# Attention of a hybrid decoder step: products of weights and values placed alternately in the two column halves of TensorE's array

## What the reference computes

```python
p_c = masked_softmax(q @ kc, ends of the 32-token blocks <= position)   # compressed keys, 32 of them
p_s = masked_softmax(q @ k_slc, keys <= position)                        # selected keys: here all blocks up to the query
p_w = masked_softmax(q @ k_win, the last 512 keys)                       # window
out = g0 * (p_c @ vc) + g1 * (p_s @ v_slc) + g2 * (p_w @ v_win)          # g: a sigmoid gate per head and branch
```

## Time and profile before

| | us |
|---|---|
| median of 3 runs | 2473.39 (2472.95 to 2475.03) |
| the profiled execution, own time | 2473.83 |
| its span | 2472.0 |
| TensorE busy with matmuls | 2288.4 (93%) |
| TensorE busy with weight loads | 1726.6 (70%) |
| VectorE busy | 826.4 (33%) |
| ScalarE busy | 501.9 (20%) |
| GpSimd busy | 292.6 (12%) |

### The profile page before, as it was taken

The page is one execution under the profiler, slowest core; times in us unless marked ns, Lnnn a source line. Parts: engine busy times, 40 slices in busy tenths (PEclk is TensorE's granted clock), DMA queues, the critical chain, the costliest instruction groups (busy, mean ns, idle before and its releaser), DMA issues.

```text
span 2472.0 us, 30188 instructions
## 1 busy us (share of the span) xinstructions
PE 2288.4 (93%) x11143; PEld 1726.6 (70%) x11143; DVE 826.4 (33%) x1909; ACT 501.9 (20%) x1029; POOL 292.6 (12%) x274
## 2 busy tenths in 40 slices
PE   4979999996888888899999999898999999989998
PEld 1245567775655566566667766678999999978886
DVE  0131123247666666653211111552111111133343
ACT  2020001011333333321111011442111111123232
POOL 0000001101000000003200001530000000035543
PEclk9989999997999999999999999999999999999999
DMA  7620100101200000035341342431111111134553
GB/s 269 224 75 26 43 17 18 35 2 69 78 4 4 4 5 4 4 96 154 113 117 57 100 119 86 161 122 52 51 48 37 51 34 51 34 120 128 179 171 103
DMA packets 179724, 189.40 MB, mean 77 GB/s; under 512 B 10069, under 2 KB 149437, under 8 KB 179198
## 3 DMA queue, kind: packets, MB, share of 16 engines
q1 hardware_dynamic: 178590, 184.12, 23.8%
q10 hardware_dynamic: 1056, 4.23, 0.5%
HBM read 173.88 MB, written 16.53 MB: 77 GB/s over the span
## 4 chain that ended last, share of the span: by engine, by line
PE 77%; DVE 11%; issue 5%; ACT 3%; DMA 3%; DVEq 0%; ACTq 0%; SPq 0%; POOL 0%; PEldq 0%
PE ps L2173 20%; PE ps L2091 14%; PE ps L1774 8%; PE ps L1790 5%; PE ps L2139 4%; PE ps L2140 4%; PE ps L2141 4%; PE ps L1742 3%; PE ps L1968 3%; DVE arena L1368 2%; PE ps L1951 2%; PE ps L1927 1%; DVE arena L1389 1%; ACT arena L902 1%; DMA arena<-in_w_out 1%
## 5 line engine op out<-in xcount | busy, mean ns | idle before, releaser
L2173 PE MATMUL ps<-h_hi,wup_hi 128*128 128x344 f32 x1056 | 340.6, 323 | 18.5 <-PE ps L2173 11.2
L2173 PE MATMUL ps<-h_lo,wup_hi 128*128 128x344 f32 x1056 | 339.3, 321 | 0.0
L2173 PE MATMUL ps<-h_hi,wup_lo 128*128 128x344 f32 x1056 | 339.0, 321 | 0.0
L2139 PE MATMUL ps<-rw_hi,ra_hi 128*128 128x512 f32 x540 | 217.7, 403 | 17.4 <-DVE rw_lo L1550 11.3
L2173 PEld LDWEIGHTS ps<-h_hi,wup_hi 128*128 128x128 f32 x1056 | 199.5, 189 | 24.8 <-issue 24.2
L2140 PE MATMUL ps<-rw_hi,ra_lo 128*128 128x512 f32 x540 | 214.1, 397 | 0.0
L2141 PE MATMUL ps<-rw_lo,ra_hi 128*128 128x512 f32 x540 | 213.5, 395 | 0.0
L2091 PE MATMUL ps<-hT,arena 128*128 128x344 f32 x704 | 211.1, 458 | 0.0
L1774 PE MATMUL ps<-arena,hT 128*128 128x386 f32 (+1 forms) x576 | 190.2, 491 | 12.1 <-DMA arena<-in_w_in 12.1
L2173 PEld LDWEIGHTS ps<-h_lo,wup_hi 128*128 128x128 f32 x1056 | 199.4, 189 | 0.0
L2173 PEld LDWEIGHTS ps<-h_hi,wup_lo 128*128 128x128 f32 x1056 | 199.2, 189 | 0.0
(11 more groups left out here) (380 smaller groups left out, 2733.4 us busy)
## 6 DMA issues: line engine op xcount, KB each, us to landing
hT<-in_w_down SPq DMA_DIRECT2D x66, 512.0 KB, 3.5
arena<-in_w_ada SPq DMA_DIRECT2D x12, 2048.0 KB, 7.9
arena<-in_w_up SPq DMA_DIRECT2D x44, 512.0 KB, 4.9
arena<-in_w_in SPq DMA_DIRECT2D x30, 512.0 KB, 4.8
arena<-in_w_out SPq DMA_DIRECT2D x24, 512.0 KB, 3.6
arena<-in_cache_cmp_kv SPq DMA_DIRECT2D x64, 128.0 KB, 2.0
arena<-in_cache_slc_kv SPq DMA_DIRECT2D x128, 64.0 KB, 1.9
arena<-in_w_in SPq DMA_DIRECT2D x4, 1544.0 KB, 9.0
```

What stands on the lines that cost most here:

```text
L2139: nc.tensor.matmul(out, ra_hi[rnd][a][:, rows], rw_hi[rnd][w][:, cols], start=(k == 0), stop=False)
L2173: ins = nc.tensor.matmul(ps[:, bank, 0:TG], w[:, k0 + k, :], h[:, k, toks], start=(k == 0 and j == 0), stop=(k == KD - 1 and j == 2))
```

## The change

In `att_PV` the products of a query block alternate between partitions 0 to 63 and 64 to 127 of the bank, counted on from the "w" unit to the "s" unit, so that the bank holds two partial sums of 64 x 128. ScalarE's `att_out` moves the upper partial sum to one of two buffers `ohalf` in SBUF; it no longer waits for the transfer of `ost`, and waits instead that the buffer has been read. VectorE has an `att_out` of its own: it waits for that move (and, for the first query block, for the transfer of `ost`), adds both halves, and writes `ost`. On VectorE it stands behind max(u + 2) of even u of 2 and more; the one of the last query block stands behind the loop over u, ahead of the next head's max(0). To keep the number of semaphores, four of the sample part's semaphores become one that counts 1 to 4, at the same places.

```diff
+        ohalf = [Pm[0:HD, 6, j * P:(j + 1) * P] for j in range(2)]
...
+        s_oh = sem("att_half")
...
@@ ScalarE
             def att_out(i, h):
 
                 act.wait_ge(s_pv, h * NU + (2 * i + 2))
-                if i == 0:
-                    act.wait_ge(s_ybd, h * 16 + 16)
-                nc.scalar.activation(ost[:, i * P:(i + 1) * P], ps[0:HD, 6 + i % 2, 0:P], ACT.Copy).then_inc(s_comb, 1)
+                act.wait_ge(s_comb, h * NT + max(i, 1))
+                nc.scalar.activation(ohalf[i % 2], ps[HD:P, 6 + i % 2, 0:P], ACT.Copy).then_inc(s_oh, 1)
...
@@ VectorE
+            def att_out(i, h):
+
+                dve.wait_ge(s_oh, h * NT + (i + 1))
+                if i == 0:
+                    dve.wait_ge(s_ybd, h * 16 + 16)
+                nc.vector.tensor_tensor(ost[:, i * P:(i + 1) * P], ps[0:HD, 6 + i % 2, 0:P], ohalf[i % 2], ALU.add).then_inc(s_comb, 1)
+
...
+                    if u % 2 == 0 and u:
+                        att_out(u // 2 - 1, h)
+                att_out(NT - 1, h)
             own.end(NH)
...
@@ TensorE, att_PV
                 if kind == "w":
                     pe.wait_ge(s_comb, h * NT + max(i, 1))
+
+                at, last = (0 if kind == "w" else len(units[u - 1][3])), len(units[2 * i][3]) + i
                 for o, (c, w, b) in enumerate(blocks):
...
-                    ins = nc.tensor.matmul(ps[0:HD, 6 + i % 2, 0:P], v, src, start=(kind == "w" and o == 0),
-                                           stop=(kind == "s" and b == i))
+                    half = (at + o) % 2 * HD
+                    ins = nc.tensor.matmul(ps[half:half + HD, 6 + i % 2, 0:P], v, src, start=(at + o < 2), stop=(at + o >= last - 1))
                 ins.then_inc(s_pv, 1)
```

More of the change, by code:

```diff
@@ L384, in build @@
             sem(n) for n in ("pages_used", "pages_weighted", "pages_T", "pages_act", "pages_dve", "q_padded"))
[L385 to L388, removed]
+        s_sps, s_Qall, s_soft, s_softm, s_softe, s_sPT, s_sPTe = (
+            sem(n) for n in ("samples_ps", "Q_all", "soft", "soft_max", "soft_exp", "sPT_ps", "sPT"))
+        s_cg, s_cge, s_sWd, s_sWp, s_sh2, s_shd, s_sCn, s_sya = (
+            sem(n) for n in ("sm_gate", "sm_exp", "sm_W", "sm_W_ps", "sm_h", "sm_std", "sm_C", "sm_ya"))
+        SP_Q, SP_Y, SP_IMP, SP_O = 1, 2, 3, 4
         s_wmg, s_wl = ([sem(f"{n}{j}") for j in range(2)] for n in ("wmerge", "w_up"))
@@ L1436, in samples_dve @@
                 if n == 1:
-                    dve.wait_ge(s_Qps, 1)
+                    dve.wait_ge(s_sps, SP_Q)
                     for g in range(NKV):
@@ L1495, in samples_dve @@
                 if n == 10:
-                    dve.wait_ge(s_syT, 1)
+                    dve.wait_ge(s_sps, SP_Y)
                     nc.vector.tensor_copy(yaT[:, :, SEQ:TOK], ps[:, 5, 256:288].rearrange("p (b h) -> p h b", h=MH)).then_inc(s_sya, 1)
@@ L1512, in samples_dve @@
                 if n == 22:
-                    dve.wait_ge(s_impps, 1)
+                    dve.wait_ge(s_sps, SP_IMP)
                     step(nc.vector.tensor_reduce(imp, ps[0:SR, 4, 0:NCMP].rearrange("p (k r) -> p k r", r=2), AX.X, ALU.add))
@@ L1539, in samples_dve @@
                 if n == 32:
-                    dve.wait_ge(s_Osum, 1)
+                    dve.wait_ge(s_sps, SP_O)
                     for h in range(NH):
@@ L2004, in samples_pe @@
                         ins = nc.tensor.transpose(ps[:, 5, 64 + j * NS:64 + (j + 1) * NS], Ps[:, lo:lo + P], ident[0:NS, 0:NS])
-                    ins.then_inc(s_Qps, 1)
+                    ins.then_inc(s_sps, 1)
                 if n == 3:
@@ L2031, in samples_pe @@
                         pe.wait_ge(s_sh2, 2)
-                        nc.tensor.transpose(ps[:, 5, 256:288], hv, ident[0:32, 0:32]).then_inc(s_syT, 1)
+                        nc.tensor.transpose(ps[:, 5, 256:288], hv, ident[0:32, 0:32]).then_inc(s_sps, 1)
                     for j in range(NPAGE):
@@ L2041, in samples_pe @@
                     pe.wait_ge(s_soft, 2)
-                    nc.tensor.matmul(ps[0:SR, 4, 0:NCMP], cst("same_group", SR), pcm, start=True, stop=True).then_inc(s_impps, 1)
+                    nc.tensor.matmul(ps[0:SR, 4, 0:NCMP], cst("same_group", SR), pcm, start=True, stop=True).then_inc(s_sps, 1)
                 if n == 24:
@@ L2071, in samples_pe @@
                 if n == 32:
-                    nc.tensor.matmul(ps[:, 0, 0:SR], ones[0:1, :], zrow[:, 0:SR], start=False, stop=True).then_inc(s_Osum, 1)
+                    nc.tensor.matmul(ps[:, 0, 0:SR], ones[0:1, :], zrow[:, 0:SR], start=False, stop=True).then_inc(s_sps, 1)
             def scores(b):
```

## The result

The change makes the kernel slower: 2513.4 us median (2510.8 to 2518.5) against 2473.2, ratio 1.0163 (1.0149 to 1.0177), or 40 us. The forecast was 2495 with a range of 2486 to 2513; the time lies 0.4 us above it. The sign, the place and the largest term were right, and the sum was short by 18 us. The profiled execution took 2510.8, its span is 2509.0, 37.0 above the span before.

What follows compares the result with a forecast made beforehand. VectorE's and ScalarE's chain of max, exp and scale was taken to bound the middle of a head. +30.1 us there less 8.6 at the heads' ends gave +21.5 on 2473.39: 2495 us, range 2486 to 2513.

Steps and rivals of the forecast that it cites:

- What bounds the stage: Middle of a head: VectorE's and ScalarE's max, exp and scale in sequence set a unit's period, whatever TensorE does.
- The hold of 3.76 us a head: Even steps 2 to 12: VectorE's wait, addition and exposed copies delay scale(u + 2), 30.1 us over 8 heads.
- Full overlap: Products in different halves run side by side, n taking n + 1 steps for 2n; chance 0.56 with nearly full.
- The move ends at 690.75 as now (same size, same place in ScalarE's order): Step u = 6: ScalarE's move behind exp(8) keeps its time, seen by VectorE at 690.78, 0.16 behind scale's old start.
- 719.25 - 718.71 = 0.54: Head's end: shorter PV(13) lets T(15) start 0.54 us earlier, limited by scale(15).
- The passage, "gain 1.01 us": Between heads: PV(15) ends 1.82 us earlier, the table load after addition and max(0) 1.01 us earlier, at 7 passages.
- The clock: Rival 3: in the middle TensorE's clock falls once a head, some 2 us lost each, 2511 in total; chance 0.07.
- The signs in the new profile: Expected in the new profile: addition waits 0.8 to 1.4 us, TensorE waits over 100, 12 matmuls about 1.0, heads 2.7 longer.
- Rival 1: The halves don't overlap: TensorE keeps its pace, VectorE pays all, +36 us, 2510; chance 0.22.
- the addition's bounds: VectorE's addition, taken as 0.20 us, lies between 0.16 and 0.30; over 48 times -2 to +5 us.

Runs made afterwards that it cites:

- the better order: Changed kernel with additions in odd steps, no ScalarE buffer wait, each head's last addition between the next head's max(0) and max(1): 2466.6 us, ratio 0.9963.

## Why the prediction was right or wrong

The mechanism was right; what failed are four sizes in the sum: the start of ScalarE's move, the gain booked to PV(13), the length of the passage behind the addition, and the clock, put at nothing.

- **What bounds the stage**: right. VectorE's and ScalarE's chain sets the middle; freed TensorE time became idle (50.87 us a head with the halves alone, 50.88 before).
- **The hold of 3.76 us a head**: right. 3.73 with everything in the lower half.
- **Full overlap**: right. 0.055 us from start to start.
- **"The move ends at 690.75 as now (same size, same place in ScalarE's order)"**: wrong. Its place in the order was the same, its partitions were not. 0.13 us later on ScalarE and 0.02 more, six times a head; with small gains in other steps the chain is 54.64 against 53.87 with everything in the lower half, 0.77 a head, 6.2 us in all.
- **"719.25 - 718.71 = 0.54"** from PV(13): wrong, 0. TensorE reached the second group of the next head's queries earlier and waited there 0.77 us for ScalarE's copy of T(14) (L934), which stands behind exp(15), as the passage above shows. T(15) follows scale(15)'s reciprocals by 1.86 us, by 1.85 before. 4.3 us.
- **The passage, "gain 1.01 us"**: of which 0.47 without PV(13); measured 0. PV(14) and PV(15) gave 1.22 of 1.28, but behind the addition the next head's max(0) starts 0.48 us later and not 0.20, as it is the loop's first instruction (0.21 where it is not, see the better order), and the table load is seen 0.18 behind the maximum and not 0.04. 7 x 0.49 = 3.4 us.
- **The clock**: it stood as a rival of its own, at 16 us and a chance of 0.07, as if it came or didn't. It came, beside the forecast, at 0.56 us a head: 4.5 us. It should have been a term of the sum.
- **The signs in the new profile**: TensorE's waits (over 100 us said, 122.9 found) and 12 matmuls (1.0 said, 0.88 found) came. The additions' waits were said to be 0.8 to 1.4 us and are 1.52 to 1.65 in the middle; rows 5 already give 1.51, from the maximum's end at 689.27 to 690.78. The heads are 5.1 us longer and not 2.7.
- Together 6.2 + 4.3 + 3.4 + 4.5 - 0.2 (the hold) = 18.2 us, from 21.5 to the 39.7 by which the stage grew in the trace. That the medians lie 40 apart while the spans of the two traces lie 37.0 apart stays open. Rival 1's 2510 came close by luck and for another reason: the products do overlap. Its own mechanism was measured at 2508.6.
- The range failed because it took in the addition's bounds and the rivals one at a time. All the mis-sized terms lay on the slow side, and each was taken at its best.

## What to carry to other kernels

Before an engine is made faster, look at what the others wait for: if the chain of maximum, exponential and scaling never waits for TensorE, faster products only lengthen TensorE's idle time. When a step must be added to the engine of that chain, the slot counts for more than its duration: the same 64 additions cost 36 us more behind a move that was queued behind exp than one step later, and next to nothing once the last of a head also stood behind the next maximum. The freed engine pays off once work of the bounding engine moves to it, here the masks, which took the kernel to 0.9876 of its time before.

## What the runs showed of the hardware

- Two neighbouring fp32 products of 64 columns, in different column halves and the same PSUM bank, overlap fully: 0.055 us from start to start on average (0.01 within a pair), against 0.114 in one half.
- ScalarE, like VectorE, gives up its overlap of neighbouring instructions when the PSUM partitions it reads from change between 0 and 64: 0.23 against 0.10 us, and 0.30 against 0.16. Here it is paid twice, going and coming back.
- The granted clock fell to its lower level (1.2 GHz) within a stage in which TensorE was never idle for more than 2.4 us at a time outside the passages: after 4 us with 2.51 busy it was 0.59. Keeping TensorE busy at one place moved the fall to another (746 to 752).
